# A two-block transformer step in fp32 on one core: the last mixer's token-pair reads, compression and interleave are moved

## What is computed

```
u = h @ w_in                              # q | kc vc | ks vs | kw vw | gates | conformer a, b
q  = rope(rms_norm(q)); ks, kw = rope(rms_norm(ks)), rope(rms_norm(kw))
kc = rms_norm(gelu(blocks(rope(kc)) @ w1[0]) @ w2[0])     # 32-token windows, stride 16
vc =          gelu(blocks(vc)       @ w1[1]) @ w2[1]
o_nsa = g0 * attend(q, kc, vc) + g1 * attend(q, ks, vs) + g2 * attend(q, kw, vw)   # 8 heads of 64
z = causal_dwconv(a * sigmoid(b), 31 taps) + bias
z = silu(layer_norm(z))
x = x + concat(o_nsa, z) @ w_out          # k-tiles 0-3 are o_nsa, 4-7 are z
```

## Time and profile before

| | us |
|---|---|
| time, median of 3 runs | 2339.42 (2338.87 to 2340.22) |
| span of the profiled execution | 2339.1 |
| TensorE (PE) matmul busy | 2277.7 |
| VectorE (DVE) busy | 1485.2 |
| ScalarE (ACT) busy | 1164.7 |
| GpSimd (POOL) busy | 128.7 |

### The profile page before, as it was taken

How to read it: one execution, slowest core, us unless ns; L and a number is a source line. 1 busy time by engine, 2 the same in 40 slices (tenths; PEclk the granted TensorE clock), 3 DMA queues, 4 the chain that set the end, 5 groups by cost and what they waited for, 6 DMA issues and landing times.

```text
span 2339.1 us, 33502 instructions
## 1 busy us (share of the span) xinstructions
PE 2277.7 (97%) x13839; PEld 1929.1 (82%) x13839; DVE 1485.2 (63%) x2139; ACT 1164.7 (50%) x1799; POOL 128.7 (6%) x197
## 2 busy tenths in 40 slices
PE   8999999999999999999999999999989999788999
PEld 7888798887888878888898877888878887666887
DVE  5665567857666556664668667666467664565663
ACT  5554346534555436553356344555344553545652
POOL 2100010120000000000000110000000001320000
PEclk9999999999999999999999999999999999889999
DMA  6756473445565556566544446566535665442663
GB/s 220 228 187 214 146 226 113 133 127 188 180 191 187 190 187 199 185 203 201 175 153 132 136 145 206 180 192 209 193 122 189 182 211 175 131 129 84 205 192 132
DMA packets 283560, 408.09 MB, mean 174 GB/s; under 512 B 13700, under 2 KB 170688, under 8 KB 283152
## 3 DMA queue, kind: packets, MB, share of 16 engines
q1 hardware_dynamic: 275600, 380.91, 51.1%
q0 software_dynamic: 7808, 25.04, 3.6%
HBM read 403.98 MB, written 1.91 MB: 174 GB/s over the span
## 4 chain that ended last, share of the span: by engine, by line
PE 86%; DVE 8%; ACT 4%; DMA 1%; issue 1%; POOL 0%; SPq 0%; DVEq 0%; ACTq 0%; POOLq 0%
PE PS L517 23%; PE PS L449 13%; PE PS L451 12%; PE PS L450 12%; PE PS L516 10%; PE PS L446 2%; DVE WL L1266 2%; PE PS L448 2%; PE PS L447 2%; PE PS L519 1%; PE PS L466 1%; ACT WH L922 1%; DVE QX L1513 1%; DMA RW<-in_w_in_odd 1%; PE PS L661 0%
## 5 line engine op out<-in xcount | busy, mean ns | idle before, releaser
L1266 DVE TENSOR_TENSOR WL<-RW,WH 128x1024 fp32r<-128x1024 f32 (+2 forms) x732 | 870.8, 1220 | 314.9 <-ACT WH L922 312.4
L922 ACT ACTIVATE WH<-RW 128x1024 fp32r<-128x1024 f32 (+2 forms) x732 | 740.6, 1044 | 389.0 <-PE PS L451 223.2
L517 PE MATMUL PS<-XT,WH 128*128 128x512 f32 x2368 | 808.4, 394 | 0.0
L516 PE MATMUL PS<-XT,WL 128*128 128x256 f32 x2072 | 580.5, 280 | 0.0
L517 PEld LDWEIGHTS PS<-XT,WH 128*128 128x128 f32 x2368 | 425.1, 188 | 76.7
L516 PEld LDWEIGHTS PS<-XT,WL 128*128 128x128 f32 x2072 | 390.0, 188 | 13.3
L449 PE MATMUL PS<-WH,HTH 128*128 128x512 f32 x688 | 271.4, 394 | 0.0
L451 PE MATMUL PS<-WH,HTL 128*128 128x512 f32 x688 | 270.8, 394 | 0.0
L450 PE MATMUL PS<-WL,HTH 128*128 128x512 f32 x688 | 269.7, 392 | 0.0
L449 PE MATMUL PS<-WH,XT 128*128 128x512 f32 (+4 forms) x640 | 252.4, 394 | 8.5 <-DVE SX L1420 3.3
L451 PE MATMUL PS<-WH,XT 128*128 128x512 f32 (+4 forms) x640 | 243.2, 380 | 0.0
(11 more groups left out here) (438 smaller groups left out, 2556.1 us busy)
## 6 DMA issues: line engine op xcount, KB each, us to landing
RW<-in_w_ff_in SPq DMA_DIRECT2D x256, 512.0 KB, 4.4
RW<-in_w_ff_out SPq DMA_DIRECT2D x128, 512.0 KB, 4.5
RW<-in_w_in SPq DMA_DIRECT2D x56, 512.0 KB, 4.5
RW<-in_w_gate SPq DMA_DIRECT2D x48, 512.0 KB, 4.2
RW<-in_ffn_gate SPq DMA_DIRECT2D x44, 512.0 KB, 4.3
RW<-in_ffn_up SPq DMA_DIRECT2D x44, 512.0 KB, 4.5
RW<-in_ffn_down SPq DMA_DIRECT2D x44, 512.0 KB, 4.6
RW<-in_w_out SPq DMA_DIRECT2D x16, 512.0 KB, 4.7
```

Source lines behind the costliest of these rows:

```text
L516: self.e.matmul(k.PS[:, b.n, 0:T], wl, k.XTH[:, kt, :], start=False, stop=False)
L517: ins = self.e.matmul(k.PS[:, b.n, :], wh, k.XT[:, kt, :], start=kt == 0, stop=kt == 7)
L922: self.e.activation(u.hi_out, raw, ACT.Copy).then_inc(*self.s["hi"].up(u.n))
L1266: self.e.tensor_tensor(u.lo_out, raw, u.hi_out.bitcast(F), ALU.subtract).then_inc(*self.s["lo"].up(u.n))
```

## The change

Four edits, all in the last mixer. (a) `e.windows()` is called right after the window projection, ahead of the q projection and of the keys' rotation. (b) The entries of both `beside` lists move up: `paired(0)` and `paired(1)` by one part, `hidden` to the last part of the q projection, `hidden_turn`, `features("k")` and `compressed_rows` by one or two parts; `compressed_keys` moves from the loop's second tick to the end of the gate projection. (c) The convolution does three steps per tick. (d) In `out_odd` the first four units are taken in the order of k-tiles, a part of token tile 1 waits for its own k-tile's item only, and the loop may call two parts of tile 1 when two of its items are done.

```diff
         for t in range(2):
             e.odd_win(t, bks[t])
             self.drop(bks[t], ("odd_a", ("win", t)))
+        e.windows()
...
-        beside = [lambda: rotate("k", 0, 8, 12, 12), e.nothing, lambda: rotate("k", 1, 8, 12, 12), e.windows, e.nothing,
-                  e.nothing, lambda: paired(0), lambda: paired(1)]
+        beside = [lambda: rotate("k", 0, 8, 12, 12), e.nothing, lambda: rotate("k", 1, 8, 12, 12), e.nothing, e.nothing,
+                  lambda: paired(0), lambda: paired(1), hidden]
...
-        beside = [lambda: rotate("q", 0, 0, 8, 8), hidden, lambda: (e.keys_double(), e.clear_vcb(), rotate("q", 1, 0, 8, 8)),
-                  hidden_turn, lambda: (features("k", 0), features("k", 1)), compressed_rows, e.nothing,
-                  lambda: features("q", 0)]
+        beside = [lambda: rotate("q", 0, 0, 8, 8), hidden_turn, lambda: (e.keys_double(), e.clear_vcb(), rotate("q", 1, 0, 8, 8)),
+                  lambda: (features("k", 0), features("k", 1)), compressed_rows, e.nothing, e.nothing,
+                  lambda: (features("q", 0), compressed_keys())]
...
-        y = self.out_odd(Operand(k.OTH, k.OTL, lambda kt, t: done[t] if kt < 4 else [("turn_lo", ("conf", t))]))
+        y = self.out_odd(Operand(k.OTH, k.OTL, lambda kt, t: (done[1][kt:kt + 1] if t else done[0]) if kt < 4 else [("turn_lo", ("conf", t))]))
...
-            if ticks == 2:
-                compressed_keys()
...
-                for _ in range(2):
+                for _ in range(3):
...
-            elif outs < 4 and len(done[0]) == 4 or outs < 8 and len(done[1]) == 4:
+            elif len(done[0]) == 4 and outs < (4, 4, 6, 6, 8)[len(done[1])]:
...
-        held = [(half, k0, self.take(wsrc(w, k0, KU, 512 * half, 512))) for half in range(2) for k0 in (0, 2)]
+        held = [(half, k0, self.take(wsrc(w, k0, KU, 512 * half, 512))) for k0 in (0, 2) for half in range(2)]
```

## The result

The changed kernel takes 2346.54 us (median of five runs, 2345.41 to 2348.57) against 2339.42 for the kernel before on the same chip (2337.13 to 2340.22): 1.0033 times as long, 95% interval 1.0023 to 1.0044. So the medians differ by 7.1 and 4.7 us, and both intervals lie clear of 1: the change costs time, by 0.1 to 0.4%. The forecast was 2344.9, range 2335 to 2350, with "slower" at 0.5.

What follows compares the result with a forecast made beforehand. PE was taken as hardly ever idle outside this mixer, with five holes inside it and a lower clock after holes. +3.0 (compression), +3.4 (convolution) and -1.0 (conformers and output) gave +5.4, so 2344.9 us, range 2335 to 2350.

Steps and rivals of the forecast that it cites:

- Steps 1 and 2: Early reads and calls queued behind `hidden` on ACT: convolution starts later, +3.0 us (bounds -0.5 and +4.7).
- Step 3: Three convolution steps per tick: more steps ahead of item 5's transposes, +3.4 us there (bounds +2.4 and +5.4).
- Step 4: Conformers' work and table loads among items 6 and 7: +12.3 at item 7's transposes, shorter tail, net +2.5 us.
- Step 5: Output parts: 9.5 instead of twelve remain behind item 7's split, -3.5 us.
- (A): Clock stays up at `hidden` and doesn't fall at the gate parts: +1.9 in all, 2341.3 us; chance 0.17.
- (B): Reads aren't earlier, PRS lands past 2009 behind the weights and delays `hidden`: 2350 us; chance 0.05.
- (C): Conformers hide in the holes of rounds 6 and 7: -6.9 in all, 2332.5 us; chance 0.15.
- (D): Convolution steps starve on DG or Z4, clock falls in rounds 6 and 7: another 3 to 6, 2349.5; chance 0.10.

Runs made afterwards that it cites:

- e1: Kernel before with only the early reads and the moved calls; 2342.88 us against 2337.54, ratio 1.0024.
- e2: Kernel before with only three convolution steps per tick instead of two; 2344.74 us against 2337.54, ratio 1.0030.
- e3: Kernel before with only the new order of the output parts; 2334.90 us against 2337.54, ratio 0.9990.
- e6: Changed kernel with the conformers taken into the loop only in tick 27; 2338.72 us against 2338.67 for the kernel before, ratio 1.0000.
- e4: Kernel before with early reads and paired transposes one part earlier, `hidden` and all behind it in their old places; 2336.93 us against 2337.54, ratio 0.9996.
- e5: Changed kernel with the q copies and q's first rotation ahead of `hidden` again; 2339.88 us against 2338.67 for the kernel before, ratio 1.0007.
- e9: Changed kernel, unaltered, timed again; 2344.07 us against 2339.35 for the kernel before, ratio 1.0021.
- e8: Kernel before, unchanged, timed against itself; 2338.72 us against 2338.67, ratio 1.0001.
- e11: e10 with the feed-forward's weight cuts issued behind tile 0's residual and norm; 2336.12 us against 2339.35 for the kernel before, ratio 0.9984.
- e10: e7 with the compressed keys copied ahead of the gates' sigmoids; 2332.59 us against 2339.35 for the kernel before, ratio 0.9970.
- e7: e4 with the new order of the output parts, two steps per tick; 2334.14 us against 2338.67 for the kernel before, ratio 0.9980.

## Why the forecast came out right, and where it didn't

**Steps 1 and 2, +3.0 at the convolution's start: right in cause, size measured +3.6** (90.8 and 93.1 against 89.3 and 87.4, means), or +3.4 with e1, e2, e3 and e6. The intermediate times hold within 1 us: `hidden` at 2016.62 (forecast 2016.2) waiting for DVE's FB, the gelu at 2025.41 (2025.7), the second q copy at about 2026.2 (2026.6), the compressed keys at 2043.3 to 2043.6 (2043.9), the first exponentials at 2049.48 (2048.9), and a wait of 2.19 for the doubled keys (3).

The holes were not right: I had PE through with the q projection at 2010.4, and it was at 2006.7. The pairs came 1.2 earlier than assumed, and the other 2.5 is the clock: I had the last two parts at the lower level as before the change, but behind a hole of 1.83 their matmuls took 0.39, not 0.63. So `hidden`'s hole is 9.94 instead of 5.8. That cost nothing more, because FB and not PE sets `hidden`'s start, and the slow restart (0.51 from 2016 to 2020) was already in the sum. e4 and e5 show the cause from both sides: with the early reads and an early `hidden`, but the q copies ahead of it, the loss is gone. I had also given the new hole at the doubled keys half a chance to cost clock. It did: the eight transposes behind the 2.19 took 1.97 instead of 1.04, at a granted clock of 0.50 (2033.6 to 2037). PE no longer waits for the compressed keys' copy, so what this adds to the stage wasn't separated.

One term was too small. I took 0.5 for weight units pushed back by the reads. The keys' rotation, which on ACT stands behind the cuts of these units, starts 22.3 to 23.2 after the first keys' copy in the four profiles without early reads (mean 22.72) and 23.1 to 24.6 in the nine with them (mean 23.85): +1.1, and +1.8 in e9. Of the +3.6 about 2.5 is then left for the order of the queues. In e9 the cut itself waits longer for its weights. ACT in e8, then in e9 (18.4 and 20.3 after the first keys' copy):

```profile
2001.62 1.06 ACT L922 ACTIVATE WH<-RW 128x1024 fp32r<-128x1024 f32 x1 [2.32 <-DMA RW<-in_w_in_odd]
```

```profile
2001.42 1.06 ACT L922 ACTIVATE WH<-RW 128x1024 fp32r<-128x1024 f32 x1 [3.21 <-DMA RW<-in_w_in_odd]
```

The rotation is ahead of FB on DVE, so this delay reaches `hidden` whole; it is 1.4 of the 2.3 by which the two profiles of the changed kernel differ at the convolution. No run has a late rotation without the early reads, and none moves the reads without the pairs, so the share of the reads is a comparison of profiles, not an experiment.

**Step 3, +3.4 at item 5's transposes: mis-sized.** From the convolution's start to item 5 it is 28.2 and 28.4 before, 30.6 and 29.2 after, 29.6 in e2 and in e5, 29.4 in e6: +1.6 in the changed kernel (mean of two), +1.2 in these three. The first profile of each kernel gives +2.4, the lower bound. PE has no wait at all between 2075.52 and item 5 in the changed kernel, so the ten steps filled all of the 2.5 us of waits before: 4.9 - 2.5 = 2.4. PE's busy time in the stretch says the same, 30.65 instead of 25.72. The 1.0 that I had added for a step at the slow clock isn't there. What takes the other profiles below 2.4 is how long the low clock lasts at the start of the stretch. In the windows of the changed kernel (columns as above) PE had hardly worked ahead of the convolution, and the clock is 0.50 from 2076 to 2080 and 0.83 in the 4 us after:

```profile
2072.00:2076.00 4.00, 0.96 (x14) 0.68 (x16) 3.69 (x16) 1.97 (x10) 0.73 (x1) 0.82 1.02 262
2076.00:2080.00 4.00, 4.00 (x33) 2.59 (x26) 2.23 (x10) 0.96 (x4) 0.94 (x2) 0.50 0.38 146
2080.00:2084.00 4.00, 4.00 (x41) 2.90 (x40) 1.22 (x3) 0.86 (x2) 1.79 (x5) 0.83 0.95 209
```

The four groups of L894 behind the first steps take 2.75 from start to start there (2078.24 to 2080.99), 2.69 and 2.75 in the two profiles of the kernel before, but 1.94 in e2, 1.68 in e6 and 1.46 in e9, where full clock is back sooner. That is 1.3 of the 1.5 by which e9's stretch is shorter than that of the first profile.

**Step 4, the conformers, net +2.5: right.** Item 5 to item 7 is 24.9 where I had 12.8 + 12.3 = 25.1, the tail behind item 7 is 4.9 and 3.7 where I had 4.1, and from item 5 to the last split it is 29.8 and 28.6 against 26.7 in both profiles before, +2.5. e2 shows the same with nothing else changed and e6 takes most of it back by delaying only the conformers. The four table loads stand in the trace where they were expected. The Trainium skill (ScalarE: Activation LUTs, What ACT_TABLE_LOAD costs) adds a drain of 1.38 us to each load; here the load at 2115.24 starts 0.02 after the cuts' end and the exponential starts 0.01 after its end, so the trace shows the 1.28 and no drain.

**Step 5, the output order, -3.5: measured -3.0, partly by balance.** From the last split to "norm" it is 15.1 instead of 18.1. The output parts behind the split shrink by more than that, from 17.2 to 12.4 us: 52 matmuls instead of 66 (2.3 parts, 3.2 us), and the hole of 2.60 is gone, behind which nine of them took 0.51 to 0.63 instead of 0.39. I had left out this slow restart, and "the residual doesn't change" was wrong and took 1.7 back. DVE of the changed kernel:

```profile
2144.76 1.23 DVE L1266 TENSOR_TENSOR WL<-RW,WH 128x1024 fp32r<-128x1024 f32 x1 [0.80 <-ACT WH L922]
2145.90 1.28 DVE L1288 SCALAR_TENSOR_TENSOR X<-X,PS 128x512 f32<-128x512 f32 x2
```

The output parts end 4.8 earlier, counted from the split, but the last cut of feed-forward weights only 3.1 (8.8 behind the split instead of 11.9). It waits for the high half on ACT, which waits 0.96 for the DMA, and the residual stands behind the cut: the hole at the last norm grows from 0.93 to 2.65. e11 closes it and pays more elsewhere.

**The sum.** +3.0 + 3.4 - 1.0 = +5.4 was forecast; the landmarks give +3.6 + 1.6 - 0.5 = +4.7 at "norm", the times +7.1 and +4.7. So the total came out partly by balance: step 3 was too large and steps 1, 2 and 5 came out a little costlier than forecast, each with misses of its own inside it. Singly timed, the parts give +5.3 + 7.2 - 2.6 = +9.9, more than the whole, with about 2.3 us of uncertainty on each; in the landmarks at "norm" they give +2.6 + 5.9 - 3.3 = +5.2. The difference of the two sums isn't explained.

**The rivals.** (A) fell: after 9.94 us of idling the clock was down at `hidden`, and it was down as well behind the shorter holes of e4 (5.18, `hidden` takes 8.99) and e11 (5.60, 8.86), which are near the 5.8 that (A) spoke of. Behind the 2.19 at the doubled keys it fell again. (B) fell: the pairs landed by 2003.28. (C) fell: item 7 came 24.9 behind item 5, not under 18. (D) fell: there is no wait for DG, and the slow clock behind new holes stays inside step 4's times: 0.50 from 2116 to 2120 (the scores at 2117.60 take 2.08, where others take 1.13), 0.71 to 2124, and item 7's outputs at 2132.92 take 1.97 instead of 1.09.

## What to carry to other kernels

A call that is moved up to fill one engine's hole takes its waiting instruction up on every other in-order queue as well. Before moving it, write down for each queue what was done in front of it and is now done behind it: here 5 us more of idling on ACT outweighed a hole on PE that an earlier read had already made shorter. Early reads can be kept and the dependent call left where it is: e4 costs nothing, and with (d) and the early keys' copy e10 is the fastest. What the reads push back belongs in the sum.

Work that uses another function table is better taken into a loop of exponentials at its end, where it needs the fewest loads (e6), even if an engine has room in the middle; e6 doesn't separate the loads from the rest of the work that moves with them. And when the parts in front of a fixed supply of weights get shorter, look at what stands behind the weights' cuts: part of the gain waits there.

## What the runs showed of the hardware that I hadn't expected

- Equal programs differ by stage more than the total suggests. From the first keys' copy to the convolution's start the kernel before took 89.3 and 87.4 us in two profiles and the changed kernel 90.8 and 93.1. The stretch behind the last landmark took 192.5 to 192.6 in most profiles and 194.1 to 194.2 in three (e5, e7, e9). This is the clock: in its first 20 us the granted clock is 0.91 in these three, with 86 matmuls, and 1.00 in the others, with 93 (e11, with its own hole, apart). One profile can't carry a claim on 2 us; a timed set of several runs or the structure of the waits can.
- After 9.94 us without work, PE's granted clock is 0.51 of full speed, 1.2 GHz, from 2016 to 2020 and 1.00 from 2020 to 2024. The 64 matmuls of `hidden` then take 8.75 us.
- The length of a short hole doesn't tell whether the clock falls. At the paired transposes the two q parts behind a hole of 2.42 ran at full clock in e1 (0.39 a matmul), and the first of them behind 2.40 at the lower level in e4 (0.63). At the last norm it fell behind a hole of 1.90 in e5 and stayed up behind one of 2.65 in the changed kernel.
